# A new order of work for the token mixer of a diffusion-transformer layer: chunks of 512 tokens, with attention, norms and projections interleaved by hand

## The chip, the cores and the metric

The kernel runs on the 8 cores of one Trainium2 chip, one sample of the batch on each core. The time of a run is the device time of its slowest core, in microseconds. Each core has five engines that run their own queues in order and meet through semaphores: TensorE (PE in the profile, its weight loads PEld), VectorE (DVE), ScalarE (ACT), GpSimd (POOL) and SyncE (SP). GpSimd's queue issues the DMAs that convert f32 weights to bf16, SyncE's queue issues the others.

## The reference

One layer is computed for 2048 latent tokens of width 1024, with 256 context tokens that give only keys and values. Cut to what matters here:

```python
h = modulate(rmsnorm(x, norm1_g), sh1, sc1)          # mod = silu(c) @ w_ada + b_ada, six vectors
b, cg, xin, q, k, v, ga, gb = split(h @ w_in)         # 512,512,512, 512,128,128, 1024,1024 columns
u  = cg * xin
ya = (b * (b_conv + sum(shift(u, j) * w_conv[j] for j in 3 taps))) @ w_a
q, k = rope(q), rope(k)                               # 8 query heads, 2 key heads of 64
yb = window_attention(q, k, v, k_ctx, v_ctx, sink) @ w_b   # blocks of 128: previous, own, next + 256 context keys
x  = x + g1 * ((sigmoid(ga) * ya + sigmoid(gb) * yb) @ w_o)
h  = modulate(rmsnorm(x, norm2_g), sh2, sc2)
x  = x + g2 * hierarchical_moe(h)                     # top-1 of 4 groups, top-2 of its 8 experts, 32 in all
out = rmsnorm(x, final_g)
```

## The kernel before, in words

The program is written as a list of operations, each for one engine with the names of what it reads and writes; a small scheduler (class `Sched`) turns these names into semaphore waits. Every engine executes its operations in the order of the program, so the order in which the Python code emits them is the order of work on each queue.

The opening loads constants, computes the modulation vectors for norm 1 from four slices of `w_ada` (`load_slot`, three buffers in turn), and stores them broadcast in `mod1`. The third of four x buffers lies on `scb`, the broadcast conditioning vector that the modulation matmuls read.

Norm 1 (`s0_dma` to `s0_apply`, `norm_apply` L346 and L348) goes over all 18 tiles of 128 tokens (16 latent, 2 context): a square sum on ScalarE, a scaled multiply and an add on VectorE in f32, eight f32 transposes on TensorE (L355) and two copies on ScalarE into `HT`, which holds the transposed activations of the whole sequence. Then keys (`k_proj`, `k_rope`) and values of all tokens are projected.

The mixer then runs twice, for the two halves of the sequence (`for half in range(2)`). In each half there are stages one after the other, each over the half's two chunks of 512 tokens: the product `cg * xin` (with one-column matmuls for the neighbour of the half's edge), conv and B, the gate `ga` with `w_a`, the queries with rope (`q_proj`, `q_rope`, L620 to L624), attention (`att_scores` L678, mask on GpSimd L684, `att_pv`, `att_tr`), the gate `gb` with `w_b`, and the output projection with the residual add (L786, L788). Each stage loads its weights again in the second half, through the three buffers. In the first half's attention, the eight remaining slices of `w_ada` are loaded and multiplied between the units (`mod2_load`, `mod2_chunk`). Every matmul group goes through the one helper at L279, so groups in the profile are told apart by their tiles.

After both halves norm 2 goes over the 16 tiles (`n2_apply`, `n2_router`), the routing is computed on VectorE, the expert loop runs over 47 blocks of up to 256 tokens with a ring of six weight buffers, and a last loop combines the experts' rows, adds and normalises.

## Time and profile before

| | |
|---|---|
| median of 3 runs | 1210.74 us (1201.68 to 1235.05) |
| the profiled execution | 1204.12 us, span of its slowest core 1202.1 us |
| spans of the eight cores | 1142.2 to 1202.1 us |
| busy time on the slowest core | TensorE 878.4, VectorE 585.6, ScalarE 407.2, GpSimd 336.0 us |
| moved by DMA | 156.22 MB, mean 130 GB/s |

All rows below are of core 1, the slowest. The span is the time from its first instruction to its last. The granted clock of TensorE is a share of 2.4 GHz; it has two levels, 1.0 (2.4 GHz) and 0.5 (1.2 GHz), and a figure between them is a mean over a stretch.

### The profile page before, as it was taken

Reading aid. Unit: us, or ns where it says so; the run is one execution under the profiler, and the core shown is the slowest. Engines: PE = TensorE matmul, PEld = TensorE weight load, DVE = VectorE, ACT = ScalarE, POOL = GpSimd, SP = SyncE. Lnnn points to the kernel's source line nnn. Section 1 sums busy time; section 2 is a strip of 40 time slices with the busy share of each in tenths; the row PEclk is TensorE's granted clock in tenths of the full one; section 3 lists DMA queues with packets and bytes.
Section 4 is the critical chain, followed back from the end, with each engine's and each line's share of the span. In section 5 each row is a group of like instructions: output and inputs, shape, how many; then the busy total and the mean of one; then the engine's idle time right before and its main releaser. Section 6 shows DMA issues by size and latency. Waiting matters only on the chain. (4 is left out here: it accounts for less than half of the span.)

```text
span 1202.1 us, 17590 instructions; the slowest of 8 cores (1142.2 to 1202.1 us)
## 1 busy us (share of the span) xinstructions
PE 878.4 (73%) x6394; PEld 534.8 (44%) x6394; DVE 585.6 (49%) x1000; ACT 407.2 (34%) x833; POOL 336.0 (28%) x348
## 2 busy tenths in 40 slices
PE   1436999977899999877995436886887787888400
PEld 0125554434654444344444314664565565666200
DVE  1258718251235555442478874342344343434498
ACT  0047321245721311288224301332333333334332
POOL 2200000025600000155000004564465565564200
PEclk9755899995589999989997556998999999999755
DMA  9995085299844742741295481599988989887474
GB/s 152 177 191 156 2 105 71 29 144 156 130 140 68 108 70 35 104 73 63 85 138 140 116 145 39 106 175 183 211 167 164 169 152 178 161 167 153 142 262 173
DMA packets 75155, 156.22 MB, mean 130 GB/s; under 512 B 16946, under 2 KB 53298, under 8 KB 70464
## 3 DMA queue, kind: packets, MB, share of 16 engines
q0 software_dynamic: 61392, 112.86, 56.7%
q1 hardware_dynamic: 13680, 42.25, 10.6%
q8 instruction: 53, 0.87, 0.3%
q14 instruction: 30, 0.25, 0.1%
HBM read 287.20 MB, written 37.22 MB: 270 GB/s over the span
## 5 line engine op out<-in xcount | busy, mean ns | idle before, releaser
L279 PE MATMUL ps<-s_HT,s_ER 128*128 128x512 bf16 (+1 forms) x1232 | 256.8, 358 | 10.6 <-DMA s_ER<-win 4.5
L279 PEld LDWEIGHTS ps<-s_HT,s_ER 128*128 128x128 bf16 x1232 | 111.6, 98 | 142.7 <-issue 16.0
L1072 DVE TENSOR_TENSOR s_MT<-ps,s_MT 128x256 bf16<-128x256 f32 x94 | 39.9, 425 | 178.2 <-ACT s_MT L1071 99.6
L279 PE MATMUL ps<-s_MT,s_ER 128*128 128x256 bf16 x736 | 95.5, 294 | 38.8 <-DVE s_MT L1058 22.1
L279 PE MATMUL ps<-s_MT,s_HT 128*128 128x256 bf16 x768 | 93.8, 284 | 36.5 <-DVE s_MT L1058 32.3
L279 PE MATMUL ps<-s_ER,s_XR 64*128 64x256 bf16 (+1 forms) x376 | 69.8, 366 | 52.5 <-DVE s_XR L300 17.7
L279 PEld LDWEIGHTS ps<-s_MT,s_ER 128*128 128x128 bf16 x736 | 76.3, 106 | 62.4 <-issue 30.8
L279 PEld LDWEIGHTS ps<-s_MT,s_HT 128*128 128x128 bf16 x768 | 76.4, 102 | 58.2 <-issue 25.9
L279 PE MATMUL ps<-s_ER,s_MT 128*128 128x512 bf16 x440 | 99.1, 379 | 0.5 <-DVE s_ER L1077 0.5
L255 POOL DMA_DIRECT2D s_ER<-win x20 | 17.5, 877 | 290.2 <-PE ps L279 276.8
L279 PE MATMUL ps<-s_ER 128*128 128x512 bf16 (+1 forms) x288 | 80.5, 389 | 15.1 <-DVE s_ER L982 10.1
L678 ACT ACTIVATE s_OV<-ps 128x512 bf16<-128x512 f32 (+1 forms) x184 | 83.3, 709 | 18.2 <-PE ps L279 18.0
L1058 DVE COPY s_MT<-ps 128x1024 bf16<-128x1024 bf16 x94 | 62.0, 687 | 55.4 <-PE ps L279 51.5
L1071 ACT ACTIVATE s_MT<-ps 128x256 bf16<-128x256 f32 x94 | 36.1, 384 | 153.3 <-PE ps L279 118.0
L1042 POOL DMA_INDIRECT s_XG<-hd,s_toki x72 | 75.4, 1047 | 23.4 <-issue 18.0
L684 POOL TENSOR_TENSOR s_OV<-s_OV,s_m 128x512 bf16<-128x512 bf16 x60 | 68.0, 1152 | 30.2 <-ACT s_OV L678 30.2
L1095 POOL DMA_INDIRECT yd<-s_OV,s_rowi x48 | 52.5, 1094 | 77.4 <-ACT s_OV L1088 67.3
L1095 POOL DMA_INDIRECT yd<-s_ER,s_rowi x46 | 50.1, 1090 | 71.9 <-ACT s_ER L1088 65.4
L279 PEld LDWEIGHTS ps<-s_ER,s_XR 64*128 64x128 bf16 (+1 forms) x376 | 25.6, 110 | 91.9 <-ACT s_OV L678 22.4
L1088 ACT ACTIVATE s_OV<-ps 128x512 bf16<-128x512 f32 x96 | 49.7, 602 | 47.9 <-PE ps L279 47.0
L355 PE MATMUL ps<-s_identf,s_XR 128*128 128x128 f32 x144 | 35.2, 426 | 38.8 <-DVE s_XR L348 18.8
L1088 ACT ACTIVATE s_ER<-ps 128x512 bf16<-128x512 f32 x92 | 47.5, 602 | 47.2 <-PE ps L279 43.3
(187 smaller groups left out, 1241.1 us busy)
## 6 DMA issues: line engine op xcount, KB each, us to landing
s_HT<-wex POOLq DMA_DIRECT2D x24, 1536.0 KB
s_ER<-wex POOLq DMA_DIRECT2D x23, 1536.0 KB
s_ER<-win POOLq DMA_DIRECT2D x19, 1024.0 KB, 11.8
s_XR<-x SPq DMA_DIRECT2D x32, 512.0 KB, 7.9
s_XR<-wada POOLq DMA_DIRECT2D x8, 1024.0 KB, 14.2
s_HT<-yd SPq DMA_DIRECT2D x16, 512.0 KB, 4.6
out<-s_XR SPq DMA_DIRECT2D x16, 512.0 KB, 2.9
s_ER<-wada POOLq DMA_DIRECT2D x4, 1024.0 KB, 31.2
```

The lines of the kernel that those rows point to most:

```text
L255: S.op("pool", lambda e, out=out, in_=in_: e.dma_start(out=out, in_=in_), reads=reads, writes=writes, dma=key)
L279: ins = e.matmul(o, lhsT=l, rhs=r, start=s0, stop=s1)
L355: ins = e.transpose(ps[bk][:, kk * 128:(kk + 1) * 128], xn[:, k * 128:(k + 1) * 128], identf[:])
L678: S.op("act", lambda e, bk=bk, p0=p0, hh=hh, w=w, npr=len(pr), Pb=Pb: e.activation(out=Pb[:, p0:p0 + npr, hh * 256:(hh + 1) * 256], in_=ps ...
L684: S.op("pool", lambda e, i=i, mk=mk, Pb=Pb: e.tensor_tensor(out=Pb[:, i, :].rearrange("p (b n) -> p b n", n=128), in0=Pb[:, i, :].rearrang ...
L1042: S.op("pool", lambda e, i=i, s=s, c_=c_: e.indirect_dma_start(out=XGb[(i % 4) * 2 + s], out_offset=None, in_=hd_d, in_offset=bass.Indirec ...
L1058: S.op("dve", lambda e, i=i, s=s, psb=psb: e.tensor_copy(out=XT[i % 2][:, :, s * 128:(s + 1) * 128], in_=psb.rearrange("p (k n) -> p k n", ...
L1071: S.op("act", lambda e, b=b, j=j: e.activation(out=sab[j], in_=ps[b][:, 0:256], func=AF.Silu), reads=[("ps", b)], writes=[("sab", j)])
L1072: S.op("dve", lambda e, b=b, j=j, i=i: e.tensor_tensor(out=acT[i % 2][:, j, :], in0=ps[b][:, 256:512], in1=sab[j], op=ALU.mult), reads=[(" ...
L1088: S.op("act", lambda e, b=b, h=h, yb=yb: e.activation(out=yb[:, h * 512:(h + 1) * 512], in_=ps[b][:], func=AF.Copy), reads=[("ps", b)], wr ...
L1095: S.op("pool", lambda e, s=s, q=q, c_=c_: e.indirect_dma_start(out=yd_d, out_offset=bass.IndirectOffsetOnAxis(ap=rowi[:, s, c_:c_ + 1], ax ...
```

## The change

The token mixer is written anew. The list of weights, the arithmetic of the layer and the order of routing, expert loop and closing norm stay; the mixer, norm 1 and norm 2 are put in another order:

- The scheduler finds dependences from the addresses that each operation reads and writes (by 4-byte column of SBUF, by bank of PSUM) instead of from names. All tiles are views of one SBUF tensor.
- Weights come in the order in which a buffer holds them, one run of bytes for each partition. Each mixer weight is loaded once, since the whole sequence passes a weight while it is there. The four first `w_ada` slices have four buffers; x has six.
- `weave(main, side)` emits two lists of steps alternately, in proportion to costs that are written beside the steps.
- Norm 1 of four tiles comes first; the other tiles are woven, chunk by chunk, into the projections of `cg`, `xin`, `k` and `v` (`cx_step`, `proj_step`, `v_step`). Its transposes are bf16. The add of every third tile is on GpSimd. Keys are projected once for both key heads.
- Queries of chunks 0 and 1 follow; then attention of chunks 0 and 1 (16 units) is woven into the remaining queries, conv and B of all chunks and the second part of the modulation; attention of chunks 2 and 3 is woven into the gates of chunks 0 and 1. A score matmul has 512 columns instead of two of 256.
- Both gates of a chunk and their sum are one step (`gate_step`), with `tanh` of half the argument in the place of `sigmoid`.
- The output projection of chunk c follows the gates of chunk c + 1. Norm 2 of chunks 0 and 1 is woven into the gates of chunks 2 and 3 (its add on GpSimd), that of chunk 2 into the last four tiles of the output projection, that of chunk 3 stands alone. The first four expert weights are asked for after the last gates.

The diff, cut to the order of work and the steps that are woven:

```diff
+def weave(main, side):
+    tm = float(sum(c for c, _ in main)) or 1.0
+    ts = float(sum(c for c, _ in side)) or 1.0
+    done_m, done_s, j = 0.0, 0.0, 0
+    for c, f in main:
+        while j < len(side) and done_s / ts <= done_m / tm:
+            side[j][1]()
+            done_s += side[j][0]
+            j += 1
+        f()
+        done_m += c
+    while j < len(side):
+        side[j][1]()
+        j += 1
...
+        sdma(badab, bada1_d.partition_broadcast(128), "c_bada")
+        sdma(ngt, ng1_d.partition_broadcast(128), "c_ng1")
+        def x_load(t):
+            src = x_d[t * 128:(t + 1) * 128, :] if t < 16 else ctx_d[(t - 16) * 128:(t - 15) * 128, :]
+            sdma(xs[t % 6], src, ("xs", t % 6))
+        for t in range(6):
+            x_load(t)
...
+        order1 = (2, 3, 0, 1)
+        for i, n in enumerate(order1):
+            gdma(wadb[i], wad_d[n], ("wad", i))
+        gdma(identb, id_d, "c_idb")
+        gdma(slotf(0), wsl_d[0], ("w", 0)); gdma(slotf(1), wsl_d[1], ("w", 1))
+        gdma(kvw.rearrange("p k n -> p (k n)"), wkv_d, "c_kv")
+        gdma(pmb, pm_d, "c_pm")
+        gdma(C2, c2_d, "c_c2"); gdma(S2, s2_d, "c_s2")
+        gdma(slotf(6), wsl_d[2], ("w", 6)); gdma(slotf(7), wsl_d[3], ("w", 7))
...
+        def n1_apply(t):
             c = 0 if t < 16 else 1
...
+            x_ = xs[t % 6]
+            stt(x_, x_, rstd[:, t:t + 1], mod1[:, 2 * c + 1, :], ALU.mult, ALU.mult, rd=[rstd[:, t:t + 1]])
+            tt(xn[t % 2], x_, mod1[:, 2 * c, :], ALU.add, eng="pool" if t % 3 == 2 else "dve")
+            if t + 6 < 18:
+                x_load(t + 6)
+            b_ = bank("misc")
+            psb = b_[:, :].bitcast(BF16)
+            x2 = xn[t % 2]
...
+            S.op("pe", fn, reads=[x2, identb], writes=[b_[:]])
+            return b_
...
+        def n1_step(t):
+            def f():
+                if t + 3 < NT:
+                    n1_sq(t + 3)
+                if t + 2 < NT:
+                    rs_a(rstd[:, t + 2:t + 3], ss[:, t + 2:t + 3])
+                if t + 1 < NT:
+                    recip(rstd[:, t + 1:t + 2], rstd[:, t + 1:t + 2])
+                prev = list(n1pend)
+                n1pend.clear()
+                n1pend.append((t, n1_apply(t)))
+                for p_ in prev:
+                    n1_copy(*p_)
+                if t in (3, 7, 11, 15, 17):
+                    for p_ in n1pend:
+                        n1_copy(*p_)
+                    n1pend.clear()
...
+        def cx_step(c, j):
+            def f():
+                w_ = cxw[j // 2]; jj = j % 2
+                bA = bank("main"); bB = bank("main")
+                mm(bA[:], [(bA[:], w_[:, k, 2 * jj * 128:(2 * jj + 1) * 128], HT[c][:, k, :], k == 0, k == 7) for k in range(8)],
+                   [w_[:, :, 2 * jj * 128:(2 * jj + 1) * 128], HT[c]])
+                mm(bB[:], [(bB[:], w_[:, k, (2 * jj + 1) * 128:(2 * jj + 2) * 128], HT[c][:, k, :], k == 0, k == 7) for k in range(8)],
+                   [w_[:, :, (2 * jj + 1) * 128:(2 * jj + 2) * 128], HT[c]])
+                act(tmpA[j % 2], bA[:], AF.Copy)
+                tt(UC[:, j, 1 + c * 512:1 + (c + 1) * 512], bB[:], tmpA[j % 2], ALU.mult)
...
+        def proj_step(w_, c, dst):
+            def f():
...
+                bA = bank("main")
+                mm(bA[:], [(bA[:], w_[:, k, :], HT[c][:, k, :], k == 0, k == 7) for k in range(8)], [w_, HT[c]])
+                act(qr[i], bA[:], AF.Copy)
+                rope_flush()
+                ropeq.append((bA, i, c, dst))
...
+        def rope_flush():
+            while ropeq:
+                bA, i, c, dst = ropeq.pop(0)
+                bB = bank("misc")
+                mm(bB[:], [(bB[:], pmb, qr[i], True, True)], [pmb, qr[i]])
+                cs = slice(c * 512, (c + 1) * 512)
+                tt(tmpA[i], bA[:], C2[:, cs], ALU.mult)
+                tt(tmpB[i], bB[:], S2[:, cs], ALU.mult)
+                tt(dst, tmpA[i], tmpB[i], ALU.add)
...
+        for c in range(4):
+            main = [(3.4, cx_step(c, j)) for j in range(4)]
+            main += [(1.9, proj_step(kvw[:, :, 0:128], c, kT[:, c * 512:(c + 1) * 512])), (1.7, v_step(range(4 * c, 4 * c + 4)))]
+            nxt = range(4 * c + 4, 4 * c + 8) if c < 3 else range(16, 18)
+            weave(main, [(1.0, n1_step(t)) for t in nxt])
...
+        mod2_load(0); mod2_load(1)
+        gdma(slotf(0), wab_d[0], ("w", 0)); gdma(slotf(1), wab_d[1], ("w", 1))
+        gdma(slotf(2), wsl_d[4], ("w", 2)); gdma(slotf(3), wsl_d[6], ("w", 3))
+        gdma(slotf(4), wsl_d[5], ("w", 4)); gdma(slotf(5), wsl_d[7], ("w", 5))
...
+        setpool("main", (0, 1, 2)); setpool("sc", (3, 4, 5))
+        for j in range(4):
+            proj_step(qw[:, :, j * 128:(j + 1) * 128], 0, QO[0][:, j, :])()
+        for j in range(4):
+            proj_step(qw[:, :, j * 128:(j + 1) * 128], 1, QO[1][:, j, :])()
...
+        def b_step(c, j):
+            def f():
...
+                ts(t_, UC[:, j, o0:o0 + 512], wcs[:, j * 3:j * 3 + 1], bcs[:, j:j + 1], ALU.mult, ALU.add, rd=[wcs, bcs])
+                stt(t_, UC[:, j, o0 + 1:o0 + 513], wcs[:, j * 3 + 1:j * 3 + 2], t_, ALU.mult, ALU.add, rd=[wcs])
+                stt(t_, UC[:, j, o0 + 2:o0 + 514], wcs[:, j * 3 + 2:j * 3 + 3], t_, ALU.mult, ALU.add, rd=[wcs])
+                b_ = bank("main")
+                mm(b_[:], [(b_[:], bw[:, k, j * 128:(j + 1) * 128], HT[c][:, k, :], k == 0, k == 7) for k in range(8)],
+                   [bw[:, :, j * 128:(j + 1) * 128], HT[c]])
+                tt(UC[:, j, o0:o0 + 512], b_[:], t_, ALU.mult)
...
+        def sc_step(u, i):
+            def f():
...
+                b_ = bank("sc")
+                kv_ = kT[kvh * 64:(kvh + 1) * 64, kc:kc + 128]
+                q_ = QO[u["c"]][kvh * 64:(kvh + 1) * 64, :, qc:qc + 128]
+                mm(b_[:], [(b_[:], kv_, q_, True, True)], [kv_, q_])
+                p_ = Pbs[u["pb"]][:, i, :]
+                act(p_, b_[:], AF.Exp, scale=0.125)
...
+                    S.op("pool", lambda e: e.tensor_tensor(out=p4, in0=p4, in1=m_.unsqueeze(1).to_broadcast([128, 4, 128]), op=ALU.mult),
+                         reads=[p_, m_], writes=[p_])
...
+        def att_steps(cs):
+            us = [u for c in cs for u in att_units(c)]
+            out = []
+            for i in range(len(us) + 2):
+                s_ = [(0.62, sc_step(us[i], k)) for k in range(len(us[i]["kts"]))] if i < len(us) else []
+                x_ = []
+                if 1 <= i <= len(us):
+                    x_.append((0.3, pv_step(us[i - 1])))
+                if i >= 2 and us[i - 2]["kvh"] == 1:
+                    x_.append((0.5, tr_step(us[i - 2]["n"])))
+                out += s_[:2] + x_ + s_[2:]
+            return out
+        main = [(2.5, mod2_step(0)), (2.5, mod2_step(1))]
+        qs = [(1.9, proj_step(qw[:, :, j * 128:(j + 1) * 128], c, QO[c][:, j, :])) for c in (2, 3) for j in range(4)] + [(0.2, rope_flush)]
+        bs = [(1.7, b_step(c, j)) for c in range(4) for j in range(4)]
+        rest = qs + bs
+        for i, s_ in enumerate(rest):
+            main.append(s_)
+            if i % 4 == 3 and 2 + i // 4 < 8:
+                main.append((2.5, mod2_step(2 + i // 4)))
+        main += [(3.0, mod2_finish)]
+        rope_flush()
+        weave(main, att_steps((0, 1)))
+        gdma(slotf(6), wo_d[0], ("w", 6)); gdma(slotf(7), wo_d[1], ("w", 7))
+        sdma(rc, rc_d, "c_rc")
+        n2_vectors()
...
+        def gate_step(c, oc):
+            def f():
+                os_ = slice(oc * 128, (oc + 1) * 128); gs = slice((oc % 4) * 128, (oc % 4 + 1) * 128)
+                tv = []
+                for (g_, w_, src) in ((ga[oc // 4], wav, UC[:, :, c * 512:(c + 1) * 512]), (gb[oc // 4], wbv, QO[c])):
+                    bG = bank("main"); bY = bank("main")
+                    mm(bG[:], [(bG[:], g_[:, k, gs], HT[c][:, k, :], k == 0, k == 7) for k in range(8)], [g_[:, :, gs], HT[c]])
+                    mm(bY[:], [(bY[:], w_[:, k, os_], src[:, k, :], k == 0, k == 3) for k in range(4)], [w_[:, :, os_], src])
+                    t_ = ta[_ta[0] % 3]
+                    _ta[0] += 1
+                    act(t_, bG[:], AF.Tanh, scale=0.5)
+                    stt(t_, t_, 1.0, bY[:], ALU.add, ALU.mult)
+                    tv.append(t_)
+                tt(mT[c % 2][:, oc, :], tv[0], tv[1], ALU.add)
...
+        def x1_load(c):
+            for t in range(4 * c, 4 * c + 4):
+                sdma(x1t(t), x_d[t * 128:(t + 1) * 128, :].rearrange("p (a n) -> p a n", n=256), ("x1", t))
+        def wo_step(t):
+            def f():
+                c, i = divmod(t, 4)
+                for h in range(2):
+                    b_ = bank("main")
+                    m_ = mT[c % 2][:, :, i * 128:(i + 1) * 128]
+                    mm(b_[:], [(b_[:], m_[:, k, :], wov[h][:, k, :], k == 0, k == 7) for k in range(8)], [m_, wov[h]])
+                    tt(wtmp, b_[:], G1[:, h * 512:(h + 1) * 512], ALU.mult)
+                    xv = x1t(t)[:, 2 * h:2 * h + 2, :]
+                    tt(xv, xv, q4(wtmp), ALU.add)
+                act(q4(junkw), x1t(t), AF.Square, accum=ss2[:, t:t + 1])
...
+        def n2_apply(t, eng):
+            def f():
+                stt(q4(t1f), x1t(t), rstd2[:, t:t + 1], q4(A2b), ALU.mult, ALU.mult, rd=[rstd2[:, t:t + 1]])
+                tt(xh[t % 2], t1f, B2b, ALU.add, eng=eng)
+                S.op("sp", lambda e: e.dma_start(out=hd_d[t * 128:(t + 1) * 128, :], in_=xh[t % 2]), reads=[xh[t % 2]], writes=[("hd", t)], dma=("hd", t % 2))
...
+        def n2_steps(c, eng="pool"):
+            ts_ = list(range(4 * c, 4 * c + 4))
+            out = [(0.5, rstd2_step(4 * c, 4))]
+            for i in range(6):
+                if i < 4:
+                    out.append((2.0, n2_apply(ts_[i], eng)))
+                if 1 <= i <= 4:
+                    out.append((1.0, n2_tr(ts_[i - 1])))
+                if i >= 2:
+                    out.append((0.5, n2_route(ts_[i - 2])))
+            return out
...
+        gs_ = lambda c: [(5.1, gate_step(c, oc)) for oc in range(8)]
+        weave(gs_(0), att_steps((2,)))
+        x1_load(0)
+        weave(gs_(1), att_steps((3,)))
+        x1_load(1)
+        setpool("main", range(6))
+        for t in range(0, 4):
+            wo_step(t)()
+        weave(gs_(2), n2_steps(0))
+        x1_load(2)
+        for t in range(4, 8):
+            wo_step(t)()
+        weave(gs_(3), n2_steps(1))
+        x1_load(3)
+        for i in range(4):
             W(i)
...
+        for t in range(8, 12):
+            wo_step(t)()
+        weave([(3.4, wo_step(t)) for t in range(12, 16)], n2_steps(2, "dve"))
+        for s_ in n2_steps(3, "dve"):
+            s_[1]()
+        W(4); W(5)
```

## Rows read from the trace of the kernel before

**Rows 1.** Busy time by stage: stretch, its length, busy per engine, clock, DMA share, GB/s.

```profile
core 1: us, PE busy (x) PEld busy (x) DVE busy (x) ACT busy (x) POOL busy (x), PEclk, DMA share, GB/s
0.00:66.80 66.80, 19.06 (x64) 7.06 (x64) 12.60 (x21) 8.15 (x14) 15.86 (x19) 0.80 1.02 170
66.80:128.20 61.40, 35.02 (x145) 28.38 (x146) 47.37 (x68) 36.35 (x81) 0.00 (x0) 0.50 0.60 146
...
154.20:197.20 43.00, 43.00 (x259) 20.35 (x257) 18.42 (x30) 7.12 (x15) 2.50 (x3) 1.00 0.63 87
...
262.00:334.00 72.00, 56.25 (x750) 36.85 (x751) 16.26 (x69) 47.66 (x109) 39.57 (x36) 0.52 0.96 138
...
517.00:565.00 48.00, 36.29 (x502) 21.34 (x503) 15.44 (x68) 43.92 (x109) 33.97 (x30) 0.93 0.15 25
...
635.40:686.00 50.60, 24.00 (x289) 22.15 (x288) 42.72 (x51) 22.49 (x27) 0.00 (x0) 0.58 0.41 120
686.00:736.80 50.80, 21.92 (x86) 11.22 (x83) 34.95 (x97) 2.37 (x5) 6.60 (x7) 0.53 0.63 108
736.80:1124.00 387.20, 311.34 (x2627) 231.81 (x2628) 153.76 (x235) 132.29 (x279) 211.49 (x224) 0.94 0.83 157
1124.00:1202.00 78.00, 1.39 (x7) 0.42 (x5) 62.58 (x80) 23.34 (x53) 3.61 (x4) 0.53 0.61 220
```

**Rows 2.** Timeline of the opening: start, duration, engine, line, operation, idle time before it.

```profile
50.80 3.63 PE L279 MATMUL ps<-s_ER,s_XR 128*128 128x512 bf16 x16 [2.32 <-DMA s_ER<-wada]
...
54.47 0.69 DVE L316 TENSOR_TENSOR s_XR<-ps,s_XR 128x512 f32<-128x512 f32 x1 [1.03 <-PE ps L279]
...
63.53 1.06 ACT L381 ACTIVATE s_OV<-s_XR 128x1024 bf16<-128x1024 f32 x1 [24.47 <-DMA s_XR<-x]
...
66.80 1.29 DVE L346 SCALAR_TENSOR_TENSOR s_XR<-s_XR,s_stat 128x1024 f32<-128x1024 f32 x1
```

**Rows 3.** DMA queues, first 60 us: packets, MB, share of 16 engines.

```profile
q0 software_dynamic: 6182, 5.74, 74.0%
q1 hardware_dynamic: 2057, 4.14, 27.4%
```

**Rows 4.** Timeline of TensorE, runs of matmuls of one shape.

```profile
146.14 8.20 PE L279 MATMUL ps<-s_ER,s_HT 128*128 128x128 bf16 x144
...
271.21 1.04 PE L279 MATMUL ps<-s_scb,s_XR 128*128 128x1 bf16 x32
...
334.60 3.78 PE L279 MATMUL ps<-s_identf,s_mod2T 128*128 128x128 f32 x16 [0.28 <-DVE s_mod2T L504]
...
380.44 27.79 PE L279 MATMUL ps<-s_ER,s_MT 128*128 128x512 bf16 x128
...
531.12 0.78 PE L279 MATMUL ps<-s_XR,s_OV 128*128 128x65 bf16 x20
```

**Rows 5.** Timeline of TensorE in the expert loop: the same 32 matmuls after gaps.

```profile
750.13 4.98 PE L279 MATMUL ps<-s_MT,s_HT 128*128 128x256 bf16 x32 [4.56 <-DVE s_MT L1058]
...
765.84 5.32 PE L279 MATMUL ps<-s_MT,s_ER 128*128 128x256 bf16 x32 [2.00 <-DVE s_MT L1058]
...
781.96 3.65 PE L279 MATMUL ps<-s_MT,s_ER 128*128 128x256 bf16 x32 [2.07 <-DVE s_MT L1058]
```

**Rows 6.** Groups by line: busy us and mean ns, then idle before and releaser.

```profile
L678 ACT ACTIVATE s_OV<-ps 128x512 bf16<-128x512 f32 x128 | 71.1, 766 | 18.2 <-PE ps L279 18.0
L684 POOL TENSOR_TENSOR s_OV<-s_OV,s_m 128x512 bf16<-128x512 bf16 x60 | 68.0, 1152 | 30.2 <-ACT s_OV L678 30.2
...
L348 DVE TENSOR_TENSOR s_XR<-s_XR 128x1024 f32<-128x1024 f32 x18 | 22.0, 1225 | 0.6
...
L568 DVE SCALAR_TENSOR_TENSOR s_OV<-s_ER,s_wcs,s_OV 128x512 f32<-128x512 bf16 x16 | 12.0, 752 | 0.6
...
L620 DVE TENSOR_TENSOR s_OV<-ps,s_XR 128x512 f32<-128x512 f32 x16 | 11.1, 692 | 4.5 <-ACT s_OV L610 3.2
...
L678 ACT ACT_TABLE_LOAD x2 | 2.6, 1283 | 0.0
```

1422 lines of the change are left out of this document (573 added, 849 removed).

## The prediction

> **What bounds the kernel now.** I read first the stages of the slowest core [rows 1], cut where the shape of TensorE's work changes. TensorE is the bound only in the middle: from 154 to 635 us it runs dense at a granted clock near 1.0 (2.4 GHz), 43.00 of 43.00 us busy in the stretch shown. Four stages before and after it are not its work. The opening (66.8 us) fills the DMA engines (share 1.02). Norm 1 (61.4 us) is VectorE's, 47.4 us busy while TensorE has a clock of 0.50 (1.2 GHz). The first half's attention takes 72 us at 0.52 (8 us of modulation matmuls in it), the second half's the same units in 48 us at 0.93: most of 24 us goes with the clock. Norm 2 (50.6 us) is again VectorE's. The routing (50.8), the expert loop (387.2) and the closing norm (78) make 516 us, in which the diff changes addresses and how dependences are found, but no instruction of weight and no order; I cost them at nothing. What would break that is a wait from the new dependence tracker, or a changed share of memory between the cores; between equal kernels I allow 1%, 4 us of the loop, either way. So all is decided before 686 us.
>
> Then the opening [rows 2, 3]: the fourth wada slice is multiplied at 50.8, but norm 1 starts only at 66.8, because the third x tile lands at 63.5 (its buffer lies on scb, which the modulation matmuls read to the end). Then the prices: TensorE's [rows 4], what gaps do to its clock [rows 5], and the other engines' [rows 6].
>
> **The opening.** The alias is gone, four wada slices have a buffer each, and one bada broadcast (1 MB) is dropped. Needed before norm 1: wada 4 MB, bada 1, ng1 0.5, and x is queued at once, 3 MB more: 8.5 MB. The two queues moved 5.74 and 4.14 MB in the first 60 us [rows 3], 165 GB/s, so about 52 us; the last slice's two groups and adds took 4.4 us after 50.8 [rows 2]. Norm 1 starts at about 57 (48 if x yields to wada, 62 if longer rows cast more slowly), not 66.8. Gain 10.
>
> **Four tiles ahead of the projections.** Per tile 1.29 + 1.22 on VectorE [rows 2, 6] and 0.3 for small operations (before, 61.4/18 = 3.4 us a tile leave 0.9 over the two), so 11, with the last transpose and copy 13 us. The projection of chunk 0 starts at 70.
>
> **Norm 1 woven into conv-input, k and v projections: the step that I believe costs.** TensorE's own work per chunk: 64 matmuls of 512 columns at 27.79/128 = 0.217 [rows 4] 13.8 us; k 1.7 (one column block serves both heads now); rope 0.2; v 32 x 0.057 = 1.8; transposes in bf16 4 x 8 x 0.057 = 1.8. With two tiles only in the last chunk: 76.7 us in all, well under the present time. But one step of the norm is stt, add, and *at once* the transposes; on VectorE it stands behind the multiply that empties the projection just issued, and on TensorE the transposes stand ahead of the next projection. So neither runs ahead: each step shows TensorE a gap of multiply 0.69 + 1.29 + 1.22 + 0.5 for handover and small operations = 3.7 us [rows 2, 6]. The trace of before shows no such loop; the gap lies between 2.5 (the two long operations alone) and 4.1 (the norm's cadence of 3.4 and the multiply). The add of every third tile goes to GpSimd. No row has it; the mask there, 512 bf16, takes 1.15 [rows 6]. Between VectorE's 1.22 and twice the mask, 2.3, I take the upper end, since the operand is twice as long: gap 4.8. Nine gaps of 3.7, five of 4.8 and 2 us for rope at chunk starts: 59 us. Gaps cost clock too: after gaps of 4.56 and 2.00 us the next 32 matmuls took 4.98 and 5.32 instead of 3.65, after one of 2.07 none was lost [rows 5]. Bursts here are as short as one projection (3.5 us), so I take 2 us for each of 14, 28 (0 if the clock holds; 77 if the stretch stays at 1.2 GHz, as norm 1 did). The context tiles' k and v add 4. Sum 76.7 + 59 + 28 + 4 = 168: chunk work ends at 238.
>
> What the row shows is that 2 us of idling can halve the clock and can leave it. The Trainium skill (TensorE: Matmul & The Clock Gate, Why this matters for your kernels) advises to leave no such gaps between bursts of matmuls; by it every gap here would be paid at the lower clock, which is the first rival's front part.
>
> **q of the first two chunks.** VectorE's three rope operations (3 x 0.69) outlast TensorE's 1.95: 8 x 2.1 = 17. At 255.
>
> **Attention of eight blocks woven into q, B, conv and mod2.** TensorE: 16 units of 5 scores (0.217), 20 products (0.78/20) and transposes, 2.0 each: 32; eight q projections 15.6; sixteen B groups 27.7; mod2 8 x 1.04; G1 3.8 [rows 4]: 87 us. ScalarE: 78 exponentials at 0.77 and small copies, about 70. VectorE: conv and B 16 x (3 x 0.75 + 0.69) = 47 [rows 6], rope 16.6, attention 15 (15.4 busy in the present 16 units [rows 1]): 79, of which 56 lie in the B part, where TensorE has 55. So the two share the bound there. Every engine queue is in order and two PSUM banks are shared by products, transposes, rope and mod2; I give the stalls 10 us (3 to 25): 97. The weight loads queued ahead of mod2's third slice (6 MB) need 38 us at 165 GB/s and have some 45, so they cost nothing; at the 120 GB/s of norm 2's stretch [rows 1] they would be 5 us late. The A2b and B2b expansions, moved here from norm 2, take 4 [rows 4]. The wo loads stand on GpSimd ahead of the next masks and wait for the last B group, which ends the weave, so they hold nobody. At 356.
>
> **Gates of chunks 0 and 1 with the other attention.** 24 matmuls a step, 5.2, and one unit, 2.0; ScalarE needs 5.5 and VectorE 3 in that time. 16 x 7.4 = 118. At 474. Tanh in the place of sigmoid is in no row; as one more 128x512 activation it lies within 0.2 of the exponential. If the two needed different tables, at 1.28 a load [rows 6], four loads a step would make ScalarE the bound: +50 in the two chunks, the same as the jam below, so that the range holds it; I take nothing, the end that the likeness to the exponential gives. The Trainium skill (ScalarE: Activation LUTs, Table sets: the hidden batching unit) lists exp and tanh in one set; by it nothing is added.
>
> **Output projection, gates of chunks 2 and 3, norm 2.** Projection 256 x 0.217 = 55; gates 16 x 5.2 = 83; norm 2 of chunks 0 and 1 inside the gates only TensorE's share, 7, with VectorE and GpSimd behind the matmuls (were that cover gone, 22). Chunk 2's norm runs beside the last four tiles on VectorE: 22.5 instead of 13.8, +9. The last x tiles are asked for only after the last gate, together with 6 MB of expert weights; the SP queue's share in the opening was 4.14 MB in 60 us [rows 3], so their 2 MB may take 29 us where 14 are covered: I take 6 (0 to 15). Chunk 3's norm is uncovered: 15.5. The stores of norm 2 queue on SP behind x loads that wait for a chunk's last gate; nobody needs them before the gathers after the routing. Sum 83 + 55 + 7 + 9 + 6 + 15.5 = 175.5: norm 2 ends at 649.5 instead of 686.
>
> **The sum.** 1202.1 - 36.5 = 1165.6 span, 1167.5 with the 2 us between span and execution time (1204.12). That execution lies 0.5% under the median of the three runs, 1210.74, so I take 1170, 3.4% less.
>
> **Rivals.**
> *Slower: the clock is never granted.* Place: the woven front and the woven attention. For it: 72 us at 0.52 in the same attention although TensorE was 56 us busy there, and a stage of short bursts at 0.50 [rows 1]. Price: the front 77 instead of 28 (+49), the attention's 87 us of matmuls at half speed, about 174 (+80): 1300. Against: the weave puts 512-column, full-height matmuls between the scores, and the second half held 0.93 on less. It decides if the granted clock of 240 to 380 us is under 0.7. Chance 0.10. Only the front: 1219, chance 0.15.
> *The weave jams.* In-order queues, the two shared banks and conv's VectorE work ahead of the attention's evacuations make 97 into 130 and 118 into 135: 1220. The mask on GpSimd ran at a steady 1.15 us beside a VectorE that read PSUM; conv now reads SBUF twice beside it. The Trainium skill (SBUF — State Buffer, Who interferes with whom) says that such a pair of instructions excludes each other for a whole instruction; no run here shows it. In rows, as a mechanism: all 30 masks' 34.5 us added to VectorE's 79 give 113 against the 97, +16, 1186. Chance of the jam with this in it 0.13.
> *The norm's gaps are hidden.* If VectorE ran ahead, the front would be TensorE's 81 us: 1083. Against it stands the order of issue. Chance 0.08.
> *It doesn't do what it says*: the same time because everything woven was hidden already. Excluded for attention (the 24 us between its halves are there to gain), possible in the front, and counted there.
>
> **How the numbers follow.** The forecast holds 0.47, with a range of its own of 1145 to 1195 from the bounds above; 0.07 is left to what I don't see, spread evenly. A measurement of this kernel tells some 2% from no change. Faster by more (under 1186): 0.40 of the forecast, the hidden gaps 0.08, a part of the jam 0.05: 0.53. Within 2%: 0.07, the front at the lower clock 0.14, the jam 0.07, the rest 0.03: 0.31. Slower: 0.16, with the first rival. The range 1105 to 1240 leaves out the hidden gaps and the slower rival.
>
> **What would show it.** Right: first norm operation near 57; in the front, TensorE's transposes released by VectorE's add, 14 gaps near 4 us, and a clock between 0.55 and 0.8; attention stages at a clock above 0.9 with TensorE over 85% busy; 516 us from the end of norm 2 to the end. Wrong: a front without those gaps, an attention stage much over 100 us, or a loop that isn't 387 us on the same core.

## The result, and the profile after

The changed kernel takes 1259.9 us (median of 4 runs, 1257.5 to 1266.3), 4.5% more than the kernel before: ratio 1.045, 95% interval 1.035 to 1.055. The forecast was 1170, range 1105 to 1240. Ratios here and below compare runs in which no die of the chip was disturbed, and the times given with them are of such runs; the rows shown of e6 and e13 are of executions in which core 1's die was disturbed, which made its expert loop some 40 us longer.

The profiled execution took 1262.3 us; its slowest core is again core 1, span 1260.6. First its busy time by stage, in the columns of [rows 1]:

```profile
core 1: us, PE busy (x) PEld busy (x) DVE busy (x) ACT busy (x) POOL busy (x), PEclk, DMA share, GB/s
0.00:103.70 103.70, 16.99 (x64) 6.88 (x64) 10.32 (x22) 8.14 (x14) 8.87 (x20) 1.00 0.78 146
103.70:120.27 16.57, 4.94 (x40) 3.92 (x41) 14.36 (x22) 7.96 (x17) 2.34 (x1) 0.53 0.39 127
120.27:274.90 154.63, 102.62 (x537) 49.84 (x536) 50.09 (x79) 33.31 (x62) 14.87 (x11) 0.82 0.14 36
274.90:291.88 16.98, 16.36 (x89) 7.60 (x85) 13.40 (x21) 5.68 (x11) 1.06 (x2) 1.00 1.01 163
291.88:406.00 114.12, 90.59 (x853) 42.45 (x853) 80.91 (x146) 50.83 (x92) 40.15 (x37) 0.88 0.55 96
406.00:420.30 14.30, 12.45 (x75) 10.93 (x75) 0.95 (x5) 4.71 (x9) 1.10 (x3) 0.56 0.84 146
420.30:552.00 131.70, 122.39 (x806) 54.85 (x806) 44.07 (x96) 63.91 (x118) 34.78 (x30) 0.99 0.08 29
552.00:702.70 150.70, 143.66 (x771) 67.49 (x768) 89.59 (x131) 50.81 (x78) 21.01 (x12) 0.99 0.29 70
702.70:733.80 31.10, 3.83 (x24) 1.68 (x24) 0.02 (x1) 0.92 (x2) 1.06 (x2) 0.65 1.01 184
733.80:761.90 28.10, 8.23 (x104) 7.22 (x104) 20.23 (x29) 9.94 (x13) 2.61 (x1) 0.50 0.24 80
761.90:803.30 41.40, 12.84 (x82) 9.51 (x82) 34.45 (x95) 3.52 (x6) 7.29 (x4) 0.65 0.06 19
803.30:1184.90 381.60, 317.85 (x2632) 233.96 (x2632) 153.96 (x235) 132.42 (x281) 208.25 (x225) 0.94 0.83 159
1184.90:1260.60 75.70, 0.01 (x1) 0.00 (x0) 62.58 (x80) 22.12 (x51) 2.56 (x3) 0.53 0.60 226
```

The stages are cut at the prediction's own steps, so the two can stand side by side (core 1, us). The cut at 406.0 is the request for the wo weights, the one at 420.3 the first matmul of the gates. One expansion, G1, which the forecast's 97 holds at 3.8, runs behind 406.0.

| step | forecast | measured |
|---|---|---|
| opening, to the first operation of norm 1 | 57 | 103.7 |
| four tiles ahead | 13 | 16.6 |
| front: norm 1 woven into conv-input, k, v | 168 | 154.6 |
| q of two chunks | 17 | 17.0 |
| attention woven into q, B, modulation | 97 | 114.1 |
| its end and the A2b, B2b expansions | 4 | 14.3 |
| gates of chunks 0, 1 with attention | 118 | 131.7 |
| output projection, gates, norm 2 | 175.5 | 209.9 |
| end of norm 2 | 649.5 | 761.9 |
| routing, loop, closing norm | 516 | 498.7 |

The forecast of norm 2's end is 112.4 us short: 46.7 in the opening, 34.4 in the tail (output projection, gates, norm 2), 27.4 in the woven attention and its end, 13.7 in the gates with attention, 3.6 in the four tiles, and 13.4 the other way in the front. What comes behind was 17 us shorter than before and gave a little back. Three waits make most of it; each is one row or a few, and all eight cores show them (78 to 80, 13 to 17 and 29 to 31 us). The timeline of the opening:

```profile
2.25 4.65 SPq L350 DMA_DIRECT2D sb<-x  x6
...
31.34 5.22 SPq L350 DMA_DIRECT2D sb<-sinkp  x1
...
81.94 0.21 ACT L364 ACTIVATE sb<-sb 128x8 f32<-128x8 f32 x1 [79.78 <-DMA sb<-sinkp]
82.17 1.28 ACT L364 ACT_TABLE_LOAD   x1
83.46 0.21 ACT L364 ACTIVATE sb<-sb 128x16 f32<-128x16 f32 x1
...
85.08 16.99 PE L357 MATMUL ps<-sb 128*128 128x512 bf16 x64 [85.08 <-DVE sb L381]
...
103.70 1.28 DVE L378 SCALAR_TENSOR_TENSOR sb<-sb 128x1024 f32<-128x1024 f32 x1
```

and the DMA issues of its first 60 us (count, KB each, median us from issue to landing):

```profile
sb<-wad POOLq DMA_DIRECT2D x4, 1024.0 KB, 26.4
...
sb<-x SPq DMA_DIRECT2D x6, 512.0 KB, 36.9
...
sb<-sinkp SPq DMA_DIRECT2D x1, 4.0 KB, 50.6
```

ScalarE's first operation is the exponential of the attention sinks, a 128x8 tile. The 4 KB for it now stand behind six x tiles and four small loads on SP's list: issued at 31.3, landed 50.6 us later. Behind that exponential in ScalarE's queue stands the SiLU (128x16, at 83.46) from which the modulation's operand is copied, so TensorE's first matmul comes at 85.1, though the wada slices had landed some 26 us after their issue. The same dependence stood in the kernel before and was visible there; its timeline of ScalarE begins so, 12.52 us of waiting that cost nothing, since the wada slices came later still [rows 2]:

```profile
14.67 0.21 ACT L298 ACTIVATE s_esb<-s_esb 128x8 f32<-128x8 f32 x1 [12.52 <-DMA s_esb<-sinkp]
```

The second and the third wait, on TensorE's and VectorE's timelines, and the DMA of the stretch 690 to 740 us:

```profile
325.76 12.19 PE L357 MATMUL ps<-sb 128*128 128x1 bf16 x108 [15.82 <-DMA sb<-wad]
```

```profile
701.44 1.28 DVE L378 SCALAR_TENSOR_TENSOR sb<-sb 128x1024 f32<-128x1024 f32 x1
...
733.82 1.22 DVE L369 TENSOR_TENSOR sb<-sb 128x1024 bf16<-128x1024 f32 x1 [31.11 <-issue]
```

```profile
q0 software_dynamic: 699, 7.61, 86.9%
q1 hardware_dynamic: 920, 1.27, 8.3%
...
hd<-sb SPq DMA_DIRECT2D x3, 256.0 KB, 37.6
```

TensorE waits 15.8 us for the third slice of the second modulation. VectorE's add of norm 2 waits 31.1 us; the row names no releaser but "issue", and what it needs is one of two output buffers, whose store was on its way for 37.6 us, with 8.3% of the DMA engines' time for its queue beside 86.9% for the expert weights.

The front went as forecast, in kind and size. From TensorE's timeline there:

```profile
162.82 1.01 PE L470 MATMUL ps<-sb 128*128 128x128 bf16 x8 [5.33 <-POOL sb L369]
163.63 8.34 PE L357 MATMUL ps<-sb 128*128 128x512 bf16 x32
175.32 0.62 PE L470 MATMUL ps<-sb 128*128 128x128 bf16 x8 [3.36 <-DVE sb L369]
175.78 5.32 PE L357 MATMUL ps<-sb 128*128 128x512 bf16 x16
...
219.57 3.65 PE L357 MATMUL ps<-sb 128*128 128x512 bf16 x16
```

Thirteen steps of norm 1 show a gap of 3.4 to 5.3 us ahead of their transposes, 52.0 us in all, released by the add. After it 16 matmuls take 5.32 us (granted clock 0.68 between 175.8 and 181.1) or 3.65 (clock 1.00 from 219.6 to 223.2): some gaps cost clock, some don't.

### The profile page after: what moved, and what is told of

Its sections match the earlier page's. It is cut to its first block and busy times, and to the rows that moved or that the text cites. A ratio compares the mean times of both kernels' runs of the same rounds, so it can differ in the third digit from the quotient of the medians.

```text
span 1260.6 us, 15879 instructions; the slowest of 8 cores (1202.1 to 1260.6 us)
## 1 busy us (share of the span) xinstructions
PE 852.7 (68%) x6066; PEld 496.3 (39%) x6066; DVE 574.9 (46%) x956; ACT 394.2 (31%) x747; POOL 345.9 (27%) x346
## 5 line engine op out<-in xcount | busy, mean ns | idle before, releaser
L357 PE MATMUL ps<-sb 128*128 128x512 bf16 (+8 forms) x4976 | 792.6, 317 | 208.9 <-DVE sb L381 136.7
L357 PEld LDWEIGHTS ps<-sb 128*128 128x128 bf16 (+2 forms) x4976 | 428.9, 105 | 551.4 <-issue 182.3
L364 ACT ACTIVATE sb<-ps 128x512 bf16<-128x512 f32 (+4 forms) x593 | 317.3, 584 | 580.2 <-PE ps L357 474.8
L369 DVE TENSOR_TENSOR sb<-ps,sb 128x256 bf16<-128x256 f32 (+4 forms) x262 | 124.6, 482 | 339.7 <-PE ps L357 172.1
L378 DVE SCALAR_TENSOR_TENSOR sb<-sb 128x1024 f32<-128x1024 f32 (+6 forms) x125 | 140.8, 1136 | 12.7 <-DMA sb<-yd 10.0
L1054 POOL DMA_INDIRECT yd<-sb x94 | 99.6, 1059 | 146.0 <-ACT sb L364 132.5
L669 POOL TENSOR_TENSOR sb<-sb 128x512 bf16<-128x512 bf16 x60 | 71.6, 1193 | 156.4 <-ACT sb L364 149.7
L1005 POOL DMA_INDIRECT sb<-hd,sb x94 | 96.7, 1028 | 61.6 <-DVE sb L896 33.6
L369 DVE TENSOR_TENSOR sb<-sb 128x512 bf16<-128x512 f32 (+4 forms) x113 | 86.8, 768 | 35.7 <-issue 31.1
L470 PE MATMUL ps<-sb 128*128 128x128 bf16 x144 | 15.6, 274 | 65.3 <-DVE sb L369 33.4
L1017 PE MATMUL ps<-sb 128*128 128x128 bf16 x752 | 50.0, 219 | 5.1 <-DMA sb<-hd,sb 4.0
L790 PE MATMUL ps<-sb 128*128 128x128 bf16 x128 | 12.3, 253 | 49.4 <-ACT sb L364 38.6
```

The lines of the kernel that those rows point to most:

```text
L357: ins = e.matmul(o, lhsT=l, rhs=r, start=s0, stop=s1)
L364: S.op("act", lambda e: e.activation(out=out, in_=in_, func=func, scale=scale), reads=[in_] + list(extra), writes=w)
L369: S.op(eng, lambda e: e.tensor_tensor(out=out, in0=a, in1=b, op=op), reads=[a, b], writes=[out])
L378: S.op(eng, lambda e: e.scalar_tensor_tensor(out=out, in0=a, scalar=s, in1=b, op0=o0, op1=o1), reads=[a, b] + list(rd), writes=[out])
L470: ins = e.transpose(psb[:, k * 128:(k + 1) * 128], x2[:, k * 128:(k + 1) * 128], identb)
L669: S.op("pool", lambda e: e.tensor_tensor(out=p4, in0=p4, in1=m_.unsqueeze(1).to_broadcast([128, 4, 128]), op=ALU.mult), reads=[p_, m_], wr ...
```

## The experiments

All start from the changed kernel. The expert loop's length differs between cores and chips (core 1: 347 to 382 us in these runs), so each run is also placed by what is ahead of it: the first ranking matmul of the routing ("ranks") and the first pass of the loop, both on core 1.

The runs are from several chips, each with the kernel before run beside them (1206 us beside the changed kernel, 1195 to 1202 on the others), and the changed kernel itself ran on one of them alone. A fall in time that is given in us below is read against its 1259.9. The ratios take the chip out: by them e1, e3, e4 and e9 gain some 23, 7, 29 and 11 us, each give or take some 15 to 20, so that the gains of e3 and e9 are not clear of the noise as times; there the rows decide. Nor are the rows of core 1 free of chance: norm 2's wait for a buffer, 31.1 us in the changed kernel, is between 22 and 32 us in the eight runs that leave it alone.

| run | time, us | ratio to before (95%) | ranks | loop starts |
|---|---|---|---|---|
| changed kernel | 1258 to 1266 | 1.045 (1.035 to 1.055) | 775.7 | 803.3 |
| e1 sinks first | 1229 to 1234 | 1.027 (1.018 to 1.035) | 750.0 | 777.7 |
| e2 weights moved in the program | 1261.7 | | 766.4 | 793.9 |
| e3 gate weights later | 1238 to 1251 | 1.040 (1.031 to 1.049) | 752.5 | 780.0 |
| e4 the three | 1210 to 1217 | 1.021 (1.009 to 1.034) | 732.2 | 759.8 |
| e5 norm 1 a step ahead | 1185 to 1193 | | 696.2 | 724.2 |
| e6 weights wait for stores | 1249 to 1266 | 1.049 (1.037 to 1.062) | 736.5 | 786.7 |
| e7 four edits | 1127 to 1128 | 0.941 (0.937 to 0.946) | 621.2 | 672.9 |
| e8 six edits | 1113 to 1125 | 0.933 (0.926 to 0.941) | 611.5 | 662.9 |
| e9 eight store buffers | 1232 to 1245 | 1.036 (1.027 to 1.045) | 742.4 | 769.9 |
| e10 six edits, buffers | 1110 to 1116 | 0.931 (0.925 to 0.936) | 623.8 | 651.6 |
| e11 no masks | 1262.6 | | 753.2 | 780.1 |
| e12 attention not woven | 1314.3 | | 823.5 | 850.8 |
| e13 weights behind x | 1112 to 1119 | 0.931 (0.926 to 0.936) | 628.4 | 657.0 |
| e14 weights behind tile 11 | 1108 to 1113 | 0.918 (0.903 to 0.934) | 622.8 | 650.6 |

In the kernel before, the loop starts at 736.8 [rows 1].

**e1, the opening.**

```diff
         sdma(ccs, cc_d, "c_cc")
+        sdma(esb, sink_d.partition_broadcast(128), "c_sink")
...
-        sdma(esb, sink_d.partition_broadcast(128), "c_sink")
         sdma(brtb, brt_d.partition_broadcast(128), "c_brt")
```

> One 4 KB load (the sinks) is asked for second instead of last but one on SP's list; nothing else changes. Theory (ScalarE's first operation, the exponential of the sinks, waits 80 us for that load, and the SiLU from which all modulation starts stands behind it in ScalarE's queue): the last of the four wada slices has landed at about 40 us, so the first matmul moves from 85 to under 25 us, norm 1 from 103.7 to about 48, the first projection from 120 to about 66, when its weights have landed; the time falls by about 50 us, to 1212. Rival (the opening is the DMA engines': 14 MB until 82 us whatever the order): the first projection still comes after 100 us and the time falls by under 15 us.

The first matmul came at 15.4, norm 1 at 48.7, but the first projection at 94.5; the loop started 25.6 us earlier, the time fell by some 29. So the sinks did hold the modulation, and the theory was half right: behind the wait stood the DMA engines. From the timeline of core 1:

```profile
89.65 1.06 ACT L366 ACTIVATE sb<-sb 128x1024 bf16<-128x1024 f32 x1 [24.23 <-DMA sb<-x]
...
90.80 1.00 ACT L364 ACTIVATE sb<-ps 128x1024 bf16<-128x1024 bf16 x1
...
93.68 1.01 PE L470 MATMUL ps<-sb 128*128 128x128 bf16 x8 [24.51 <-DVE sb L369]
```

The first row is the squares of the seventh x tile (e8's expectation calls it the eighth), asked for at 51.3, when the first tile has left its buffer. They wait for a load that shares the engines with 2 MB of weights for q and B, not needed before 250 us. The copy that puts the third tile into `HT`, and that the first projection needs, stands right behind them in ScalarE's queue: the pattern of the sinks again, which no run took away. Asking for the weights a chunk later (in e8) brought the first projection from 88.1 (e7) to 79.1.

**e2 and e6, the weights against the stores.**

```diff
         x1_load(3)
-        for i in range(4):
-            W(i)
...
-        W(4); W(5)
+        for i in range(6):
+            W(i)
```

> The first four expert weights (6 MB) are asked for behind the last step of norm 2, with the fifth and sixth, instead of ahead of the output projection of chunk 2. Theory (norm 2's store of a tile lands 37.6 us after its issue because it shares the DMA engines with the weights, and the second next tile needs its buffer): the stall of 31 us on VectorE ends, norm 2 ends near 731 instead of 762; the expert loop waits a little for its first weights, 0 to 8 us; the time falls by 23 to 31 us, to about 1235. Rival (the weights only move their wait to the loop, which takes 1.5 MB every 8.2 us at a DMA share of 0.83): the loop is 25 us or more longer and the time stays within 8 us of 1260.

Nothing moved: GpSimd's queue has no work between the last gate and the routing, so it runs ahead and asks for four weights at 666 us, as the changed kernel did at 672. The place in the program is not the time of issue. (The ranks come 9 us earlier in this run because its wait for the buffer was 23.2 us, within the spread named above.) In e6 the same six loads are also declared readers of the last store:

```diff
-                gdma(r_, wex_d[n], ("wr", i % NRING))
+                gdma(r_, wex_d[n], ("wr", i % NRING), reads=[("hd", 15)] if i < 6 else ())
```

> The first six expert weights wait for the last store of norm 2 (moving them in the program alone did not change when GpSimd's queue asked for them). Theory (the 31 us in which VectorE's add waits is the store ahead of it, which shares the DMA engines with 9 MB of weights): the stall falls under 3 us, norm 2 ends some 29 us earlier, the loop starts some 29 us earlier and has its first weights in time, the whole falls by 20 to 29 us, to about 1235. Rival (the weights are then what is late): the routing's end or the first pass of the loop waits for a weight, and the loop to its end is 20 us or more longer, so that the time stays within 8 us of 1260.

The stall went: the ranks came 39 us earlier than in the changed kernel (some 3 us of it are an earlier opening and a shorter wait for the modulation's slice in that run). But the loop started only 17 us earlier, since now TensorE's first pass waits for the gathered tokens:

```profile
786.66 1.89 PE L1016 MATMUL ps<-sb 128*128 128x128 bf16 x16 [26.73 <-DMA sb<-hd,sb]
```

Both theories were half right: the store had been late because of the weights, and weights that come later delay the next small transfer.

**e3, the second modulation.**

```diff
-        gdma(slotf(2), wsl_d[4], ("w", 2)); gdma(slotf(3), wsl_d[6], ("w", 3))
-        gdma(slotf(4), wsl_d[5], ("w", 4)); gdma(slotf(5), wsl_d[7], ("w", 5))
...
                     mod2_load(n + 2)
+                if n == 5:
+                    gdma(slotf(2), wsl_d[4], ("w", 2)); gdma(slotf(3), wsl_d[6], ("w", 3))
+                    gdma(slotf(4), wsl_d[5], ("w", 4)); gdma(slotf(5), wsl_d[7], ("w", 5))
```

> The four gate weights (4 MB), needed at 427 us, are asked for after the sixth step of the second modulation instead of ahead of its third slice. Theory (the third slice stands behind 6 MB, and TensorE waits 15.8 us for it): with 2 MB ahead of it the wait falls to under 2 us, and the time by about 14 us, to 1246. Rival (the weave has VectorE as its bound, 54 of 56 us busy after the wait, so VectorE, which is idle in the wait, has nothing to catch up on and the wait shows elsewhere, as a wait for the gate weights at 427): the time falls by under 5 us.

The wait before the third slice is gone (0.75 us left, for VectorE), nothing waits for the gate weights, and the time fell by about 12 us: the theory, shown by the rows rather than by the time. The loop starts 23 us earlier, since the opening and the wait for the buffer were shorter too in this run (2.9 and 7.4 us).

**e4, the sum of the three.**

> The three edits in one kernel. If the three waits stand one after the other, as the trace shows them, their gains add: 50 + 27 + 14 = 91 us, 1170, which is the time predicted for the change. If they overlap or uncover the same DMA traffic (an earlier front meets its weights later), the sum is 20 us or more short of that: 1190 or above.

1210 to 1217, not 1170, because e1 gave 29 instead of 50 and e2 nothing; what e1 and e3 gave alone, 29 and 12, nearly makes it (1219; by the ratios 23 and 7 against 29).

**e5, the order of issue in the front.**

```diff
                 n1pend.clear()
-                n1pend.append((t, n1_apply(t)))
+                if t + 1 < NT:
+                    n1_apply(t + 1)
+                n1pend.append((t, n1_turn(t)))
```

(`n1_turn` holds the transposes, which were the second half of `n1_apply`.)

> The changed kernel with one edit: a step of norm 1 issues the scaling and the add of the next tile, and the transposes of this tile, whose add went out a step before. Theory (the front's 154.6 us are 102.6 of TensorE and 52 of gaps that come from the order of issue, and part of the 102.6 is the lower clock in which it works after each gap): the gaps of 3.4 to 5.3 us fall under 1 us, the clock of this stretch rises from 0.82 to above 0.95, the front takes 82 to 100 us, and the time falls by 55 to 70 us, to about 1200. Rival (something else spaces the steps: the two shared PSUM banks, the squares on ScalarE, the arrival of x): the gaps move to another releaser and the front stays above 135 us.

The time fell by some 70 us (64 by the ratios of its two runs), to below the runs of the kernel before on the same chip (1194 to 1201). The front, then q, by stage:

```profile
121.30:202.40 81.10, 79.17 (x534) 42.20 (x533) 50.35 (x78) 33.32 (x62) 14.93 (x11) 0.99 0.32 75
202.40:219.50 17.10, 16.52 (x89) 7.73 (x86) 13.48 (x22) 5.63 (x11) 1.06 (x2) 1.00 1.02 165
```

81.1 us instead of 154.6, with the same busy VectorE (50.35 for 50.09): 52 us of gaps and the clock's share of 102.6 - 79.2 = 23 us. The prediction had put TensorE's own work there at 81 (76.7 + 4), the gaps at 59 and the clock at 28. What is left of gaps is under 0.9 us, where GpSimd's add (2.34 us) is waited for.

**e7, e8: together.** e8 has two more edits:

```diff
-        gdma(slotf(6), wsl_d[2], ("w", 6)); gdma(slotf(7), wsl_d[3], ("w", 7))
...
         for c in range(4):
+            if c == 1:
+                gdma(slotf(6), wsl_d[2], ("w", 6)); gdma(slotf(7), wsl_d[3], ("w", 7))
...
-        rest = qs + bs
-        for i, s_ in enumerate(rest):
-            main.append(s_)
-            if i % 4 == 3 and 2 + i // 4 < 8:
+        for i in range(8):
+            main += [qs[i], bs[2 * i], (0.2, rope_flush), bs[2 * i + 1]]
+            if i < 6:
```

> The sink load second on SP's list, the gate weights after the sixth modulation step, norm 1 a step ahead, and the expert weights after norm 2's last store, in one kernel. If each takes its own stall: 26 (as its own run showed) + 14 + 60 + 27 = 127 us less than the changed kernel, 1133, and faster than the kernel before by some 6%. If the earlier front only meets its x tiles or weights later, 1160 or above.

> The same, with two more edits: the weights of q and of B (2 MB, needed after 250 us) are asked for a chunk later, so that the opening's 14 MB are 12, and in the woven attention each query projection stands beside two B groups (instead of eight queries first and sixteen B groups after), since VectorE is the bound in the B part (53.8 of 56 us busy) and has time to spare in the query part. Theory: the wait for the eighth x tile (24 us with the sink load first) falls by 10 to 12 us, the woven attention by 6 to 10, so 18 us less than the kernel with four edits, 1115. Rival (VectorE's and ScalarE's sums over the whole weave, 81 and 57 of 115 us, are already spread; ends are set by the attention's chain): the weave keeps its 115 us, and the two kernels differ by 12 us or less.

e7 took 1127, as the sum had it, and beat the kernel before by 5.9%. Of e8's two edits only the load order paid (9 us to the first projection); the weave, from its table load to the request for wo, took 97.8 us in e7 and 96.8 in e8, so spreading the queries gave 1: there the rival was right. Both kernels still lose 28 us ahead of the loop, as e6 did (e8, TensorE):

```profile
662.94 1.89 PE L1022 MATMUL ps<-sb 128*128 128x128 bf16 x16 [28.13 <-DMA sb<-hd,sb]
```

**e9, e10: buffers in place of waiting.**

```diff
-        xh = [view(T0 + 12288 + i * 2048, 1024, BF16) for i in range(2)]
+        xh = [view(o_, 1024, BF16) for o_ in (P0 + 2048, P0 + 4096, P0 + 6144, P0 + 8192, OT0, Z1 + 4608, T0 + 12288, T0 + 14336)]
```

(and `t % 8` for `t % 2` where `xh` and its stores are named)

> The changed kernel with one edit: norm 2's output tile has eight buffers in turn instead of two (in memory that the attention has left), and the expert weights are asked for early, as in the changed kernel. Theory (the stall of 31 us is the wait for a buffer whose store is among the weights; the weights themselves are in nobody's way there, while behind norm 2 they delay the gathers of the first tokens, as the run with weights after the stores showed: stall gone, but 50 us instead of 28 from the ranks to the loop): no wait above 5 us in norm 2, the ranks 29 to 31 us earlier than in the changed kernel, still 28 us from there to the loop, and the time falls by about 30 us, to 1230. Rival (the stores stay late, and the gathers, which need all of them, wait in place of VectorE): the ranks move, the loop's start does not, and the time stays above 1250.

> The kernel with six edits, with the eight buffers in the place of the weights' wait for the stores. Theory: the 28 us that its loop waits for the first gathered tokens are gone but for some 4, and the loop has its weights early: 20 to 25 us less than 1118, 1095. Rival (in the loop the DMA engines are the bound, and 9 MB moved ahead of it do not shorten it): 1110 or above.

e9's loop starts 33 us earlier (some 7 of them from an earlier opening and a shorter wait for the slice), with 27.5 us from the ranks to it, no wait for a buffer is left, and the time fell by about 20 us (11 by the ratios): the wait was one for a buffer. Not all of it went; a second wait stood behind (VectorE of e9):

```profile
707.67 0.69 DVE L369 TENSOR_TENSOR sb<-sb 128x512 f32<-128x512 f32 x1 [10.13 <-DMA sb<-x]
```

That is the term "the last x tiles, 6 (0 to 15)" of the prediction, uncovered. In e10 it is 12.8 us, and so its loop starts 11 us earlier than e8's and not 24; 1110 to 1116 is the rival's number; that the DMA engines bound the loop, its reason, no run tested.

**e13, e14: the last x tiles.** Both hold back the first four weights, e13 until the last x tile has landed, e14 until tile 11 of the output projection is done:

```diff
-                gdma(r_, wex_d[n], ("wr", i % NRING))
+                gdma(r_, wex_d[n], ("wr", i % NRING), reads=[x1t(15)] if i < 4 else ())
```

and in e14, where the four calls also stand behind tile 11 in the program:

```diff
+                gdma(r_, wex_d[n], ("wr", i % NRING), reads=[ss2[:, 11:12]] if i < 4 else ())
```

> The kernel with six edits and eight buffers; the first four expert weights now wait until the last x tile of the output projection has landed. Theory (with the stores out of the way a second wait stands in the same place, 12.8 us for the last x tile, which was asked for with the weights and shares the DMA engines with them): x lands some 13 us after its issue, no wait above 4 us is left in norm 2, the ranks come 13 to 17 us earlier (at about 608 on core 1 instead of 624), and the time falls by 10 to 15 us from 1112, to 1100. Rival (weights that start 13 us later meet the gathers of the first tokens or are late in the loop): the loop starts less than 5 us earlier, or the time stays above 1107.

> As the run before, but the weights wait for the sum of squares of tile 11 instead of the x tile itself. (There x had landed 10.5 us after its issue, but the weights were declared readers of the x tile, which the next operation overwrites, so that VectorE then waited for the weights' landing: the edit put a wait of its own, 13.7 us, in the place of the one it took away.) Theory: no wait above 4 us is left in norm 2, the ranks come at about 608 on core 1 instead of 624, and the time falls by 10 to 15 us from 1112, to 1100. Rival (weights that start 15 us later meet the gathers of the first tokens or are late in the loop): the loop starts less than 5 us earlier, or the time stays above 1107.

e13 spoiled itself: x landed 10.5 us after its issue, but the edit made VectorE wait 13.7 us for the weights. In e14 VectorE waits for nothing over 0.2 us between 556 and 580 us, where e10 has its 12.8, and norm 2 ends at 596 on core 1. The loop still starts at 650.6, 1 us earlier than in e10, because the routing now waits, for the last stores (its scratch lies where they read):

```profile
616.92 0.69 DVE L902 TENSOR_TENSOR sb<-sb 128x512 f32<-128x512 f32 x1 [13.05 <-DMA hd<-sb]
```

That is the rival's outcome, if not quite its reason: it had named gathers and late weights, and it was stores. 9 MB at the 184 GB/s of the row at 702.70 are some 50 us of full DMA engines, and between the last gate and the loop there is a chain of small transfers (x, stores, gathers); wherever these runs put the weights, some of it waited.

**e11, masks and conv.** `if mk is not None:` became never true in `sc_step`, so the 60 mask products are left out.

> The changed kernel without the 60 mask multiplications of the attention on GpSimd (the window of the attention is then not masked at its edges; the rest is computed as before). Theory (a mask on GpSimd and a conv operation on VectorE, both from and to SBUF, hold each other up): conv's two multiply-adds take 0.75 to 0.78 us instead of a mean of 0.96, its first operation 0.55 instead of 0.68, so that VectorE, the bound of the B part, needs 9 us less, and the woven attention is 6 to 10 us shorter. Rival (the durations vary for another reason, PSUM or DMA traffic): the same means, and the weave shorter by under 3 us.

VectorE's conv operations, in the changed kernel and in e11:

```profile
L378 DVE SCALAR_TENSOR_TENSOR sb<-sb 128x512 f32<-128x512 bf16 x32 | 30.8, 963 | 1.1
...
L375 DVE TENSOR_SCALAR sb<-sb 128x512 f32<-128x512 bf16 x16 | 10.9, 679 | 0.0
```

```profile
L378 DVE SCALAR_TENSOR_TENSOR sb<-sb 128x512 f32<-128x512 bf16 x32 | 24.1, 752 | 1.1
...
L375 DVE TENSOR_SCALAR sb<-sb 128x512 f32<-128x512 bf16 x16 | 8.6, 538 | 0.0
```

The durations are as the theory had them: 9.0 us of VectorE's time is the masks' doing, not the 34.5 that the prediction's rival added. (Conv without masks beside it took the same 752 in the kernel before [rows 6].) The weave, less its wait for the slice, was 89.5 us instead of 98.4 on core 1, but 98.9 instead of 99.2 on core 7, where TensorE had a granted clock of 0.81 between 350 and 400 us instead of 0.86 and 1.00. What the masks cost in time stays open, with one run of e11.

**e12, the weave itself.** `weave(main, side)` became `main` followed by `side`, three times.

> The changed kernel with the attention units behind the work that they are woven into (16 units after q, B and the second modulation; 8 units after each of the two chunks of gates). Theory (weaving hides nearly all of the attention): the stretch from the first query of the weave to the first gate grows from 135 us to 170 or more, the gates with their attention from 125 to 140 or more, and the time rises by 50 to 80 us, to about 1325. Rival (the weave only trades TensorE's idle time for stalls in queues): both stretches stay within 15 us and the time below 1285.

Stage by stage (main; then 16 attention units alone; then the gates of two chunks, each with its 8 units behind it):

```profile
288.40:376.00 87.60, 56.87 (x436) 26.72 (x432) 57.80 (x96) 5.37 (x9) 3.17 (x6) 0.86 0.67 116
378.30:444.00 65.70, 58.78 (x421) 27.23 (x420) 12.76 (x50) 45.11 (x86) 35.63 (x32) 0.50 0.03 4
444.00:601.30 157.30, 147.90 (x840) 69.78 (x839) 45.34 (x96) 65.94 (x122) 34.99 (x30) 0.79 0.14 40
```

The one run took 54 us more, and the loop starts 47 us later. The third row begins with the A2b and B2b expansions; cut there in the changed kernel too (at 414.2), the first weave takes 156 us instead of 122 (a wait for the slice that is 4 us longer is in it) and the second 157 instead of 138: about what the theory had added, 35 and 15 us or more. The attention alone runs at 1.2 GHz, though TensorE is 59 of 66 us busy; woven, the stages have 0.88 and 0.99. That is no rule for attention by itself: in the kernel before, the second half's 16 units, not woven either, had 0.93 in 48 us [rows 1]. What decided between the two no run shows.

## Why the prediction was wrong

The direction was wrong because of steps that count transfers; those that count engine work came within 14 us each.

1. **The opening: the step that failed most.** "Norm 1 starts at about 57" came from bytes over bandwidth, for those bytes that norm 1 needs. It left out that ScalarE's queue is in order and starts with an operation whose 4 KB the change had put behind x. Measured 103.7; e1 shows 26 us of the time to be the order of that one load, and e8 another 9 to be 2 MB asked for too early. The bytes alone would have been about right: with the sinks first, norm 1 starts at 44 to 50. But the next line of the forecast, the first projection at 70, would still have failed: it stands at 94.5 in e1 and at 79.1 in e8, since norm 1's later tiles share the DMA engines with the weights.
2. **"Nobody needs them before the gathers", of norm 2's stores, was false.** The next but one tile needs the buffer. The prediction had named the queue and who waits for the data, and forgot who waits for the space. 31 us; e6 and e9 take that wait away in two ways. The x tiles, costed at 6, would have been 10 to 13 without it (e9, e10).
3. **The third modulation slice, costed at nothing.** "6 MB in 38 us, cover 45" was mis-sized: 8 MB were ahead of it, the two first slices among them, and it is a ninth; from 263.9 us to its landing at 325.7 are 62 us (152 GB/s, near the 165 that the prediction took). The cover was right: TensorE wanted it at 309.9, 46 us after the first issue. 15.8 us, and e3 takes them away.
4. **The end of the weave, 14.3 instead of 4 and G1's 3.8.** The row that priced the A2b and B2b expansions at 4 [rows 4] is one vector's 16 matmuls; they are two vectors, 7.6 by that row, and took 6.1 (414.2 to 420.3). The rest is G1 and the last units of the attention, with nothing woven beside them; the clock is 0.56.
5. **Front: right in mechanism and within 8% in size** (154.6 for 168; gaps 52 for 59, clock 23 for 28), shown by e5. The rivals there fell: the gaps are not hidden, and the clock is 0.82, not 0.5. Just this step was also the largest thing to gain, and the prediction took it as given.
6. **The weave: 97 forecast, 98.4 measured** without the wait for the slice (114.2 from table load to the request for wo, less 15.8), or some 102 with G1, which the forecast includes. The jam did not come. The exclusion of VectorE and GpSimd that the prediction quoted from the Trainium skill (SBUF — State Buffer, Who interferes with whom) shows in part: 9 us of VectorE's time (e11), where the rival priced all 34.5 us of masks. Gates with attention took 132 for 118: TensorE was busy for 122 us of them and idle for 9. Tanh brought no table load beside the exponential between 293 and 570 us.
7. **Routing, loop and closing norm, costed at no change, were 17 us shorter** on core 1 (498.7 for 516). The traces show where 11.2 of these are, in the routing's 32 matmuls with a mask of 256 columns each, before and after:

```profile
711.70:729.80 18.10, 13.54 (x32) 4.89 (x32) 8.63 (x32) 0.00 (x0) 0.39 (x1) 0.50 0.27 58
```

```profile
790.10:797.00 6.90, 6.40 (x32) 4.96 (x32) 6.50 (x33) 0.00 (x0) 0.00 (x0) 0.71 0.00 1
```

Before, each of them starts some 0.57 us after the last; after, they run on. The new scheduler lets one TensorE operation follow another without a wait on a semaphore (`if do["eng"] == "pe" and e == "pe"`, then `continue`), which the prediction did not look at. That this is the reason is argued, not shown: no run changes that line alone. The loop was 5.6 us and the closing norm 2.3 us shorter, and no run here tells why.

What the prediction said would show it wrong did so: norm 1 not near 57, the attention stage above 100, and a loop of 381.6 us and not 387.

Without the first three (46.7, 31.1 and 15.8 us), the rest of the forecast would have come out within 2 us, and that is luck: the gates and the end of the weave, 24 us too low, are made up for by the front and what lies behind norm 2, 31 us too high.

The edits, put together, make the kernel 7% faster than the one before (e10: 0.931, 0.925 to 0.936), once five things in the changed order are put right: two places in lists of loads, one load asked for later, the order of issue in the front, and buffers. That is more than was forecast, but not by the forecast's reasons alone: e5's 64 to 70 us are a cost that the prediction had counted and accepted. Without that edit e10 would be at some 1175 to 1185, an estimate from the two runs and close to the 1170.

## What to carry to other kernels

When loads are put in a new order, follow each small one to the operation that needs it and to what stands behind that operation in its engine's queue; a wait that is hidden in the old trace (12.5 us, harmless) is a wait that the new order can lengthen. Ask of each store who needs its buffer, not only who needs its data. Where a stage mixes large prefetches with a chain of small transfers, look at what the next small transfer will be before moving the prefetch: here each move (e6, e10, e14) moved the wait, and no run found a place where it went.

## What the runs showed that was not expected

A 4 KB load, behind 3 MB on its own queue, took 50.6 us and a 256 KB store 37.6 us to land beside large transfers of another queue, whose share of the DMA engines' time was 67 to 87%; asked for second (e1) the load took 2.7 us, and the store takes 2.0 us in the median over the whole run. The Trainium skill (DMA: Bandwidth & Descriptors, Queues, rings and completion order) says that an engine goes round the queues that have work, a packet of one at a time; the rows agree in kind, and show what it costs a queue of small packets: 920 of them had 8.3% of the engines' time, 699 of the other queue 86.9%. Dense attention with its short matmuls stayed at a granted clock of 0.50 for 66 us in e12 with TensorE 89% busy, and the same units between wider matmuls had 0.88 to 0.99. With the masks gone (e11), TensorE had no idle time on core 7 between 350 and 400 us, and its granted clock there was 0.81; on core 1 it was 0.93 and 1.00. One run does not tell whether the masks had to do with it.
